# One product over 96 rows for the router's shift, in place of four diagonal products a half

## What is computed

```
h2 = rms_norm(x, p['norm2_w']) * (1 + sc2) + sh2
x = x + g2 * expert_choice_moe(h2, p['router_w'], p['exp_w_gate'], p['exp_w_up'], p['exp_w_down'])
```

## Time and profile before

| | |
|---|---|
| time, median of 3 runs | 2164.18 us (2163.78 to 2165.16) |
| the profiled execution | 2168.93 us |
| its span | 2167.1 us |
| mean granted clock | 0.987 |
| PE / DVE / ACT busy | 2106.2 / 1692.8 / 1133.3 us |
| stage of the rows, layer 0 | from 835.52 to 850.97 us of the span |
| experts, layer 0 | from about 861 to 1150 us |

### The profile page before, as it was taken

One profiled execution on the slowest core, in us unless ns is written; L12 is line 12 of the kernel. 1 busy time (PEld: TensorE's weight loads), 2 busy tenths in 40 slices (PEclk: granted clock), 3 DMA queues, 4 the chain that ended last, 5 costly groups with the idle time before them and its releaser, 6 DMA issues.

```text
span 2167.1 us, 35863 instructions
## 1 busy us (share of the span) xinstructions
PE 2106.2 (97%) x13292; PEld 1709.2 (79%) x13292; DVE 1692.8 (78%) x2515; ACT 1133.3 (52%) x1790; POOL 160.9 (7%) x184
## 2 busy tenths in 40 slices
PE   7999999999999998999998999999999999999999
PEld 3448999999667997666667999999776999666666
DVE  6868777876778554999998778887778764799997
ACT  3534445333722144888884444433551325788884
POOL 1010000000000100111100000000100100111110
PEclk8999999999999998999999999999999999999999
DMA  9683333221332526999992233322404443999995
GB/s 394 241 303 109 115 139 134 90 79 64 127 117 101 170 93 240 397 382 383 386 371 108 91 139 129 120 79 78 151 11 166 150 136 146 357 372 385 384 384 221
DMA packets 75792, 435.77 MB, mean 201 GB/s; under 512 B 9037, under 2 KB 9773, under 8 KB 34686
## 3 DMA queue, kind: packets, MB, share of 16 engines
q1 hardware_dynamic: 54336, 352.87, 42.4%
q0 software_dynamic: 18384, 72.28, 10.7%
q10 hardware_dynamic: 2926, 8.64, 1.0%
HBM read 384.92 MB, written 48.84 MB: 200 GB/s over the span
## 4 chain that ended last, share of the span: by engine, by line
PE 82%; DVE 7%; ACT 4%; issue 3%; DVEq 2%; DMA 1%; ACTq 0%
PE ps L725 20%; PE ps L962 18%; PE ps L1307 9%; PE ps L1333 5%; PE ps L1311 4%; PE ps L904 3%; PE ps L1337 2%; PE ps L830 2%; PE ps L764 2%; PE ps L1034 2%; PE ps L1159 1%; PE ps L1162 1%; PE ps L918 1%; PE ps L1087 1%; PE ps L1064 1%
## 5 line engine op out<-in xcount | busy, mean ns | idle before, releaser
L725 PE MATMUL ps<-front_r 128*128 128x320 f32 x2432 | 417.0, 310 | 1.6 <-DVE back_r L2452 0.8
L725 PEld LDWEIGHTS ps<-front_r 128*128 128x128 f32 x2432 | 370.0, 188 | 3.0 <-DVE back_r L2452 1.4
L1405 ACT ACTIVATE front_r<-ring 128x1024 fp32r<-128x1024 f32 (+1 forms) x216 | 182.6, 846 | 261.4 <-PE ps L725 172.1
L962 PE MATMUL ps<-back_r,front_r 128*128 128x320 f32 x1728 | 265.1, 309 | 0.0
L962 PEld LDWEIGHTS ps<-back_r,front_r 128*128 128x128 f32 x1728 | 256.4, 188 | 0.0
L1405 ACT ACTIVATE back<-ps 128x512 f32<-128x512 f32 (+5 forms) x206 | 98.8, 496 | 266.9 <-PE ps L725 114.0
L962 PE MATMUL ps<-front_r 128*128 128x320 f32 x1296 | 204.7, 311 | 5.0 <-DVE back L2131 4.7
L962 PEld LDWEIGHTS ps<-front_r 128*128 128x128 f32 x1296 | 192.0, 188 | 10.1 <-DVE back L2131 9.2
L1405 ACT ACTIVATE front_r<-back 128x512 fp32r<-128x512 f32 (+2 forms) x216 | 150.1, 709 | 87.4 <-PE ps L962 35.9
L2566 DVE TENSOR_TENSOR back_r<-front,back_r 128x1024 fp32r<-128x1024 f32 x128 | 153.5, 1221 | 12.5 <-ACT back_r L1405 10.7
L1307 PE MATMUL ps<-back_r 128*80 128x512 f32 x384 | 152.3, 397 | 3.7 <-ACT back_r L1405 3.7
(11 more groups left out here) (313 smaller groups left out, 3749.6 us busy)
## 6 DMA issues: line engine op xcount, KB each, us to landing
ring<-in_stream SPq DMA_DIRECT2D x186, 1024.0 KB, 7.1
front<-in_stream SPq DMA_DIRECT2D x80, 1024.0 KB, 15.9
back<-in_stream SPq DMA_DIRECT2D x48, 1024.0 KB, 14.5
gates<-back SPq DMA_DIRECT2D x24, 640.0 KB, 3.1
back<-gates POOLq DMA_DIRECT2D x48, 320.0 KB, 3.3
kspec<-back POOLq DMA_DIRECT2D x20, 512.0 KB, 7.0
front<-kspec POOLq DMA_DIRECT2D x8, 1024.0 KB, 7.8
rows<-front ACTq DMA_DIRECT2D x10, 520.0 KB, 5.3
```

Of the source, the lines that this page charges most:

```text
L725: mm = pe.matmul(tokh(b)[:, c0:c1], w(wp)[:, k, :], src(hp, k)[:, c0:c1], start=first, stop=last)
L962: mm = pe.matmul(ps[:, bank, 0:TH], w[:, wp, k, :], x(k), start=k == 0 and wp == 0 and x is hi and j not in (2, 6), stop=k == 3 and wp == ...
L1405: return act.activation(o, i, ACT.Copy)
```

## The change

The shift is added with one product a half, over 96 rows, in fp32r. The stationary operand holds the spread root three times as 32 rows each: high, low, high. The moving operand `spread_rows` holds, for each group g and block k, a row per (k, g) with the shift of that block, zero for the others: high parts against the first two, the low part against the third. These rows are made so:

- ScalarE, after the last `late_add` of o = 0, copies the 16 columns of the shift eight times side by side into `shift_cols` (128 x 128).
- TensorE turns them with one f32 product of 128 columns behind `router_shift`'s 32 products, into PSUM bank 7.
- ScalarE copies the result to `shift_rows` (fp32r), and VectorE subtracts for rows 64 to 95 the high part, behind the `lbias` copies.
- VectorE spreads them over the blocks under the mask `sel16`, two operations on 96 x 1024, ahead of chunk 3's residual in the output projection.
- VectorE makes the low part of the root's rows 32 to 63 from PSUM, after the softmax and ahead of the copy of the turned affinities. `add_shift(0)` waits for this.
- The 16 diagonal matrices on ScalarE are gone, as are two unused semaphores.

```diff
+                        pe.wait_ge(sh_hi, 2 * l + 1)
+                        pe.matmul(ps[:, 7, 0:P], shift_cols, ident[:], start=True, stop=True).then_inc(r_lg, 1)
...
-                    for i in range(4):
-                        mm = pe.matmul(ps[:, 4 + n % 2, P * i:P * i + P], spr[:, P * t:P * t + P],
-                                       diag[:, int(t > 0), 4 * hf + i, :], start=False, stop=i == 3)
-                    mm.then_inc(t_ready, 1)
+                    pe.matmul(ps[:, 4 + n % 2, :], spr[0:96, P * t:P * t + P],
+                              spread_rows[0:96, int(t > 0), 4 * hf:4 * hf + 4, :].rearrange("p i n -> p (i n)"),
+                              start=False, stop=True).then_inc(t_ready, 1)
...
-                pe.wait_ge(z_ready, l * Z_IN + Z_IN)
+                pe.wait_ge(rt_lo, 3 * l + 3)
...
+                        act.wait_ge(r_lg, 2 * l + 1)
+                        copy(shift_rows, ps[:, 7, 0:P]).then_inc(sh_hi, 1)
                         act.wait_ge(y_sum, l * 4 + 1)
...
+                    if o == 0:
+                        act.wait_ge(modcol_read, conv_mods(l, o)[-1] + 1)
+                        copy(shift_cols.rearrange("p (j m) -> p j m", j=8), mod[:, l, 24:32, :].rearrange("p k g -> p (k g)")
+                             .unsqueeze(1).to_broadcast([P, 8, 16])).then_inc(sh_hi, 1)
...
-                        act.activation(diag[:, g, k, :], ident[:], ACT.Identity, scale=mod[:, l, 24 + k, g:g + 1])
...
                         dve.wait_ge(r_lg, 2 * l + 1)
+                        dve.wait_ge(sh_hi, 2 * l + 2)
...
+                        dve.tensor_tensor(shift_rows[64:96, :], ps[64:96, 7, 0:P], shift_rows[64:96, :].bitcast(F32),
+                                          ALU.subtract).then_inc(rt_lo, 1)
...
+                    if c == 3:
+                        whole = [96, KC, P]
+                        for g in range(2):
+                            ins = dve.tensor_tensor(spread_rows[0:96, g], shift_rows[0:96, :].bitcast(F32).unsqueeze(1).to_broadcast(whole),
+                                                    sel16[0:96, g:16:2].unsqueeze(2).to_broadcast(whole), ALU.mult)
+                        ins.then_inc(rt_lo, 1)
...
+                dve.wait_ge(z_ready, l * Z_IN + Z_IN)
+                dve.tensor_tensor(spr[32:64, :], spread_at(l, 1)[32:64, :], spr[32:64, :].bitcast(F32),
+                                  ALU.subtract).then_inc(rt_lo, 1)
```

More of the change, by code:

```diff
@@ L154, in build @@
         rw = sb("rw", [P, KC, NE])
+        with nc.sbuf_tensor("shift_rows", [P, QK], F32R) as shift_place:
+            pass
+        shift_rows = shift_place[:, P:2 * P]
         qkw = sb("qkw", [P, QK])
+        shift_cols = qkw[:, 2 * P:3 * P]
         cs = sb("cs", [P, KC, 32])
@@ L261, in build @@
         sgin, mtmp = region(106, [4, T]), region(116, [2, T])
-        z, spr, diag = region(56, [KC, T]), region(86, [T]), region(76, [2, KC, P])
+        z, spr, spread_rows = region(56, [KC, T]), region_r(86, [T]), region_r(76, [2, KC, P])
         rws, lbias = region(139.5, [2, KC, 2 * NE]), qkw[:, 0:NT * NE].rearrange("p (t e) -> p t e", t=NT)
@@ L303, in build @@
         modrow_sb, modcol_ready, modcol_read = sem("modrow_sb"), sem("modcol_ready"), sem("modcol_read")
-        f_stt, f_mm, f_arg, f_sin, f_win, f_winread = sem("f_windowed"), sem("f_mm"), sem("f_arg"), sem("f_sin"), sem("f_win"), sem("f_winread")
+        f_stt, f_mm, f_arg, f_sin, f_win = sem("f_windowed"), sem("f_mm"), sem("f_arg"), sem("f_sin"), sem("f_win")
         f_dec, f_hi, f_lo = sem("f_dec"), sem("filter_operand_hi"), sem("filter_operand_lo")
@@ L348, in build @@
         scattered, yo_free, acc_in, e_xt = sem("scattered"), sem("yo_free"), sem("acc_loaded"), sem("e_xt")
-        e_up, e_silu, e_hid, e_t, e_hidT, e_yev, e_ycev = (sem(n) for n in (
-            "e_up", "e_silu", "e_hid", "e_t", "e_hidT", "e_yev", "e_ycev"))
+        sh_hi, rt_lo = sem("shift_rows_hi"), sem("shift_and_root_lo")
+        e_silu, e_hid, e_t, e_hidT, e_yev, e_ycev = (sem(n) for n in (
+            "e_silu", "e_hid", "e_t", "e_hidT", "e_yev", "e_ycev"))
         e_xhi, e_xlo = sem("e_x_hi"), sem("e_x_lo")
@@ L1143, in router_shift @@
                             for k in range(KC):
-                                mm = pe.matmul(ps[:, 7, 320 + NE * g:320 + NE * g + NE],
+                                pe.matmul(ps[:, 7, 320 + NE * g:320 + NE * g + NE],
                                                mod[:, l, 24 + k, g:g + 1].to_broadcast([P, P]), rw[:, k, :],
                                                start=k == 0, stop=k == KC - 1)
-                        mm.then_inc(r_lg, 1)
+                        pe.wait_ge(sh_hi, 2 * l + 1)
+                        pe.matmul(ps[:, 7, 0:P], shift_cols, ident[:], start=True, stop=True).then_inc(r_lg, 1)
                     def inverse(kt, tiles):
```

## The result

The kernel after is slower: 2170.98 us median (2166.15 to 2176.70, 20 runs) against 2165.02 us (2162.04 to 2169.25, 20 runs), ratio 1.0027, 95% interval 1.0021 to 1.0034, which is 4.5 to 7.4 us. The forecast was 2163.6 us and no measurable change; rival 2, the clock, had 0.15 and 2170.0 us.

A forecast was written before the change was run, and what follows sets the result against it. TensorE was taken to hold 82% of the chain, with VectorE's search as floor under the rows' stage. Rows -1.21, late search +0.2, added products +0.44 sum to -0.57 us: 2163.6 us, range 2160.5 to 2168.0.

The forecast's parts named there:

- rival 2: Modulation items behind the rows: lighter TensorE load drops its clock; two slow items a layer give 2170.0 us; chance 0.15.
- TensorE is still busy two thirds of the time: New rows' stage: argument against a falling clock, from 0.67 us of TensorE work in each 1.0 us.
- at 1.2 GHz it would be busy throughout: New rows' stage: argument that low-clock rows would fill TensorE's time, as at the old rows' start, followed by clock 1.00.
- ScalarE's pace: Rows' stage: ScalarE needs about 2.0 us a pair of halves, so TensorE finishes near 848 us, about two before the search ends.
- The gain in the rows' stage: Both layers' rows: fewer products save 0.73 and 0.48 us, together 1.21, limited by the search; its later start costs 0.2.
- The subtraction: VectorE, between softmax and search: 0.82 us, mostly in idle time, delaying the search by 0.1 us a layer.
- The hand-over from the search's end to the places: End of the rows' stage: two small TensorE transposes before VectorE takes the places, 0.5 us, bounds 0.18 and 0.74.
- The addition in the convolution: Behind router_shift's products: one f32 product in TensorE's chain, 0.22 us a layer, 0.44 in all; bounds nothing or 0.5 a layer.
- The cover there: Convolution: VectorE's 1.91 us of idle time hides its wait and subtraction; without it 0.5 us a layer.
- The spreads: Output projection: two VectorE operations, 2.46 us, hidden in a 3.81 us wait for chunk 3 with 1.3 us to spare.
- The gathers: Behind the rows: first gather about 2.5 us earlier, but TensorE gets nothing from it.
- Rival 3: Experts' ramp: earlier rows and gathers start expert loads some 2.5 us earlier; 2161.1 us, or some 2159; chance 0.10.

The follow-up runs named there:

- after_again: The kernel after, unchanged, timed again against the kernel before on the same chip: ratio 1.0034.
- before_mods_filled: The kernel before plus unread f32 filler products in the modulation items' gaps and behind the first turn_rows, against the kernel before: ratio 1.0005.

## Why the prediction was wrong

**The step that failed** is the weighing of rival 2, "The clock falls", at 0.15: the forecast's sum put the price of the clock behind the rows at nothing, "Granted clock 1.00 from 841 to 858 us". The runs showed half clock in the modulation items instead, 11.08 us of items against 9.10 before in the mean of six layers, 4 us for both layers together. The mechanism and the place were those of rival 2. The two reasons that I had set against it are the failure. "TensorE is still busy two thirds of the time" was about right (9.18 of 14.57 us in layer 0's rows) and did not keep the clock: it fell at 848.1 us in the wait behind them. The second, "at 1.2 GHz it would be busy throughout", was nearly right too (9.30 of 10.30 us in layer 1), but there the clock stayed at 0.50 for 10.3 us, against 3.4 us at the start of the old rows, and when it had come back it held for 6.8 us, with TensorE busy 4.40 us of them.

**The price of rival 2** was too high for one item, and its total came near by luck. It has 1.6 us an item; the traces show 1.15. All four items at half clock cost 3.4 us (after_again's layer 0, 12.46 against 9.10), not 6.3; that this is less than four times 1.15 fits the wait for ScalarE, 2.07 and 1.64 us before and 0.60 after. The 2170.0 us were reckoned with two slow items in each layer; measured are three to four of them in four of six layers, at the lower price.

**ScalarE's pace**, 2.0 us a pair against 1.74 in layer 0, was mis-sized too. It made that layer's rows end at 845.9 instead of 848 us and the idle wait 4.27 us instead of about two; I had counted that time as free, since nothing waits for TensorE there. But the loss does not hang on this: in layer 1 the wait was 1.68 us, about as forecast, and layer 1 is where the clock fell and the items took 11.6 us or more in all three profiles.

**The gain in the rows' stage**, forecast at 1.21 - 0.2 us for both layers, did not appear. From the first transpose to the first item both kernels have a mean of 16.06 us over six layers. Three parts make that up:

- From the search's start (L2541) to L1278 it takes 12.20 to 12.22 us in all six layers after: the search is the floor. Before (L2519 to L1273) it took 12.95 and 12.70 us in the profile that the prediction read, which gives its 0.73 and 0.48, but 12.39 to 12.68 in the other four layers. The mean gain is 0.41 us a layer.
- The search starts 0.27 us later behind the first transpose (2.74 against 2.47). The subtraction accounts for about 0.1 of it, as forecast: the search begins 0.87 or 0.88 us behind the softmax in five of the six layers, which is the subtraction's 0.82 us and the gaps around it, against a mean of 0.78 before. In layer 0 of the first profile, at half clock, L1266 came later still, 1.16 us. The rest is the softmax, which varies by more than that from layer to layer.
- From L1278 to the first item it takes 1.24 us where the clock had already fallen (layer 0 in all three profiles) against 0.97 at full clock, 0.14 in the mean.

The hand-over from the search's end to the places took 0.64 us in layer 0 and 0.48 in layer 1, where I had 0.5.

**The addition in the convolution** was under-sized. The chain there, in answer to the earlier trace rows:

```profile
636.24 3.48 PE ps L1149 x32
639.72 0.36 PE ps L1153 x2
640.08 8.52 PE ps L1165 x16
```

0.36 us for the product in the chain, not 0.22, and 0.32 in layer 1, 0.7 us for both; within the bound of 0.5 a layer. **The cover there held**, in answer to the earlier trace rows; the timeline of the kernel after:

```profile
640.12 0.28 ACT L1410 ACTIVATE shift_rows<-ps 128x128 fp32r<-128x128 f32 x1 [14.13 <-PE ps L1153]
...
640.82 0.29 DVE L2449 TENSOR_TENSOR shift_rows<-ps,shift_rows 32x128 fp32r<-32x128 f32 x1
643.49 0.69 DVE L2454 TENSOR_TENSOR back<-ps,back 128x512 f32<-128x512 f32 x1 [2.38 <-PE ps L1165]
```

VectorE still waits 2.38 us for L1165 behind the new operation. **The spreads are hidden**, as forecast, with 1.54 us to spare where I had 1.3; in answer to the earlier trace rows:

```profile
796.62 2.35 DVE L2499 TENSOR_TENSOR back_r<-shift_rows,sel 96x1024 fp32r<-96x1024 f32 x2
800.51 1.01 DVE L1929 SCALAR_TENSOR_TENSOR X<-ps,mod,X 128x128 f32<-128x128 f32 x2 [1.54 <-PE ps L730]
```

The diagonal matrices that are gone gave nothing that shows, as said: from router_shift's products to the first transpose the mean is 199.6 us after and 199.0 before, over six layers that scatter from 197.3 to 200.6.

**The gathers** were forecast 2.5 us earlier and came 0.4 us earlier in layer 0, 855.20 against the 855.62 of the earlier trace rows, and over the six layers each not earlier at all: 20.3 us behind the first transpose after, 20.0 before. The rows' DMAs are issued earlier but take longer to land, a median of 7.6 us behind the issue against 5.3 before; the DMA engines are at a share of 1.00 in this stretch. Rival 3 had nothing to start from.

**What adds up, and what doesn't.** By the six layers each the stretch is 40.22 us after and 38.66 before, 1.56 a layer, 3.1 for both; the convolution adds 0.7. That is 3.8 of the 4.5 to 7.4 us of the timed runs. The stretch that the profiles show is a small sample, as the clock falls in a different pattern in every execution; the 0.7 us or more that is left was not placed. The cause itself is shown from four sides: light rows without any addition give 1.0025, the additions without light rows 0.9998, filler that computes nothing brings the change back to 1.0002, and the clock of all timed runs is lower exactly where the time was lost without filler. What in the light rows makes the clock fall, the gaps or the wait, stays open.

## What to carry to other kernels

Before taking work off TensorE in a stage that another engine bounds, ask what its clock does behind that stage: here seven of eight records a half taken away bought idle time, and the next light stage paid with 2 us a layer in the mean. Where only the wait grows, price the next stage at both clock levels, by rows of each level, and give that case a real chance. And look at several executions: one profile of each kernel showed totals 0.4 us apart where the medians are 6 us apart.

## What the runs showed that was not expected

- Filler products for nobody restored the time: sixteen fp32r products a layer, about 3.7 us of TensorE work by the 0.23 us each of the earlier trace rows, and the kernel is some 5 us faster than without (1.0002 against 1.0027).
- A full clock through the whole ramp into the experts (before_mods_filled) shortened that stretch by about 1.8 us a layer against the mean before, and the kernel by nothing that can be measured (0.9996 to 1.0014).
- Transposes hold the clock at least in part (1.0010 against 1.0027 and 1.0034 without them), and by the mean clock of the timed runs as well as products do (0.9842 and 0.9845).
- The clock can fall in a stage of TensorE's work without a long pause: in layer 1 it fell at 1851.6 us, at the end of the first item's rows, with no wait of TensorE above 1.68 us in the 6.8 us before.
- The rows' DMAs, issued earlier into a stretch with a DMA share of 1.00, land in 7.6 us (median) against 5.3 before; the first gather moved by almost nothing.
